# A routed block's rows stored unnormalised, with their reciprocal roots beside them

## The reference

```python
def rmsnorm(x, g):
    xf = x.astype(jnp.float32)
    y = xf * lax.rsqrt(jnp.mean(xf * xf, axis=-1, keepdims=True) + EPS)
    return (y * g.astype(jnp.float32)).astype(x.dtype)

x = x + hierarchical_moe(rmsnorm(x, norm2_g), ...)      # then a last rmsnorm

def expert_block(args):
    e, rows_tok, rows_w = args
    xb = tok[rows_tok]                       # rows of the normed x, chosen by the router
    a = xb @ w_gate[e]
    u = xb @ w_up[e]
    y = (jax.nn.silu(a) * u) @ w_down[e]
    return (y * rows_w[:, None].astype(y.dtype)).astype(tok.dtype)
```

## Time and profile before

| | |
|---|---|
| median of 3 runs | 1619.41 us (1617.6 to 1621.46) |
| time of the profiled execution | 1620.07 us |
| its span | 1618.3 us |
| PE busy | 1515.8 us (94%) |
| DVE, ACT, POOL busy | 662.3, 512.4, 473.8 us |
| read from HBM | 302.84 MB |
| weight chunks of 2048 KB to the arena, the ring, hT | 49, 43, 1 |

### The profile page before, as it was taken

How to read it: one execution, slowest core, us unless ns; L and a number is a source line. 1 busy time by engine, 2 the same in 40 slices (tenths; PEclk the granted TensorE clock), 3 DMA queues, 4 the chain that set the end, 5 groups by cost and what they waited for, 6 DMA issues and landing times.

```text
span 1618.3 us, 18890 instructions
## 1 busy us (share of the span) xinstructions
PE 1515.8 (94%) x7408; PEld 1010.7 (62%) x7409; DVE 662.3 (41%) x1090; ACT 512.4 (32%) x912; POOL 473.8 (29%) x250
## 2 busy tenths in 40 slices
PE   7999999999999999999998999898799998998986
PEld 6975566887778888878866766456344343433432
DVE  3155565223643333321135678573423232232324
ACT  5236566222543333321245433424111111111112
POOL 4441114444434444444424363432100000000100
PEclk9999999999999999999999999999799999999998
DMA  7323001222232223223223221118899999999994
GB/s 301 110 96 90 2 1 36 96 91 91 79 116 98 98 94 102 91 92 99 96 79 111 96 73 67 51 54 336 355 429 427 430 430 430 426 429 429 422 429 183
DMA packets 44680, 306.12 MB, mean 189 GB/s; under 512 B 6272, under 2 KB 6400, under 8 KB 31920
## 3 DMA queue, kind: packets, MB, share of 16 engines
q1 hardware_dynamic: 39664, 290.56, 46.2%
q0 software_dynamic: 4352, 12.25, 2.0%
q10 hardware_dynamic: 576, 2.10, 0.4%
HBM read 302.84 MB, written 4.19 MB: 190 GB/s over the span
## 4 chain that ended last, share of the span: by engine, by line
PE 73%; DMA 11%; DVE 9%; ACT 3%; issue 2%; POOL 0%; SPq 0%; ACTq 0%; DVEq 0%; POOLq 0%
PE banks L402 26%; PE banks L1059 11%; DMA ring<-experts 11%; PE banks L432 10%; PE banks L1087 3%; PE banks L2175 3%; PE banks L923 2%; PE banks L412 2%; PE banks L2104 2%; PE banks L2120 2%; PE banks L1094 2%; PE banks L780 1%; PE banks L2087 1%; PE banks L781 1%; PE banks L2091 1%
## 5 line engine op out<-in xcount | busy, mean ns | idle before, releaser
L365 POOL TENSOR_TENSOR arena_r<-ring,arena_r 128x1024 fp32r<-128x1024 f32 x143 | 352.1, 2467 | 449.9 <-ACT arena_r L350 449.9
L402 PE MATMUL banks<-hT_r,arena_r 128*128 128x512 f32 x1216 | 388.7, 391 | 5.4 <-POOL arena_r L365 4.0
L350 ACT ACTIVATE arena_r<-ring 128x1024 fp32r<-128x1024 f32 x143 | 150.7, 1059 | 466.8 <-PE banks L402 305.0
L402 PE MATMUL banks<-arena_r 128*128 128x512 f32 x800 | 293.0, 391 | 0.0
L402 PEld LDWEIGHTS banks<-hT_r,arena_r 128*128 128x128 f32 x1216 | 228.2, 188 | 59.5 <-issue 9.2
L1059 PE MATMUL banks<-ring,arena 128*64 128x512 f32 x720 | 226.1, 616 | 19.9 <-DMA ring<-experts 17.0
L432 PE MATMUL banks<-arena_r 128*128 128x512 f32 x784 | 188.3, 394 | 2.2 <-POOL arena_r L365 1.8
L1059 PEld LDWEIGHTS banks<-ring,arena 128*64 128x64 f32 x720 | 73.0, 142 | 157.0 <-issue 157.0
L432 PEld LDWEIGHTS banks<-arena_r 128*128 128x128 f32 x784 | 147.0, 188 | 38.1 <-POOL arena_r L365 3.5
L402 PEld LDWEIGHTS banks<-arena_r 128*128 128x128 f32 x800 | 150.2, 188 | 32.9
L1670 DVE TENSOR_TENSOR resid<-resid,banks 128x1024 f32<-128x1024 f32 x64 | 75.2, 1217 | 139.5 <-PE banks L1094 139.5
(11 more groups left out here) (435 smaller groups left out, 1888.1 us busy)
## 6 DMA issues: line engine op xcount, KB each, us to landing
arena<-experts SPq DMA_DIRECT2D x49, 2048.0 KB, 16.4
ring<-experts SPq DMA_DIRECT2D x43, 2048.0 KB, 16.3
ring<-stream SPq DMA_DIRECT2D x162, 512.0 KB, 3.7
ring<-experts SPq DMA_DIRECT2D x4, 1024.0 KB, 9.4
resid<-x ACTq DMA_DIRECT2D x4, 512.0 KB, 5.7
grow<-grows POOLq DMA_DIRECT2D x4, 512.0 KB, 6.8
rows<-arena POOLq DMA_DIRECT2D x4, 512.0 KB, 11.4
hT<-experts SPq DMA_DIRECT2D x1, 2048.0 KB, 16.1
```

The source lines that it names most:

```text
L350: nc.scalar.activation(parts(name, m)[:, 0, :], tile(tile_n), ACT.Copy).then_inc(S["w_high"], 1)
L365: nc.gpsimd.tensor_tensor(w[:, 1, :], tile(tile_n), plain(w[:, 0, :]), ALU.subtract).then_inc(S["w_low"], 1)
L402: last = nc.tensor.matmul(pb[:, bank, :], w[:, a, k * P:(k + 1) * P], b[:, k, :], start=(k == 0 and part == 0), stop=(k == ND - 1 and part ...
```

## The change

The rows are stored as they are in X, so ACT's scaling into `xn` is left out and POOL stores tile i as soon as `wo2_x` says that it is summed. The reciprocal roots go to a second tensor in HBM, `row_rstd`, 4 bytes for each token, in four stores. Each gather of a block's rows is followed by a gather of its roots into one of two columns, `rstd_at[q]`. ACT gives that column as the scale of the activation, DVE as the scalar of the product. Since the two columns are used in turn, clearing for block b waits for the hidden rows of block b - 2. The first gather waits for eight stores in place of four.

As `xn` is no longer written, place 2 is filled right behind chunk 4. Two waits of SP are gone: the one for the selection ahead of place 1, and the one for the first gather ahead of the places 2 and 3. The signal `xz_ready` becomes one more step of `pool_chain`, and a 64-word buffer becomes one of 48.

```diff
-            pool.wait_ge(S["xz_ready"], 1)
+            pool.wait_ge(S["pool_chain"], 6)
             low_pool(pool, "out2", 2)
 
+            def rstd_out(i):
+
+                pool.wait_ge(S["norm_xn"], 3 * NT + i + 1)
+                pool.dma_start(row_rstd[i * P:(i + 1) * P, :], rms_columns("n4", i)[2]).then_inc(S["rows_st"], 16)
+
             for i in range(NT):
-                pool.wait_ge(S["row_ready"], i + 1)
-                pool.dma_start(rows[i * P:(i + 1) * P, :], xn[:, i, :]).then_inc(S["rows_st"], 16)
+                pool.wait_ge(S["wo2_x"], i + 1)
+                pool.dma_start(rows[i * P:(i + 1) * P, :], X[:, i, :]).then_inc(S["rows_st"], 16)
+                if i:
+                    rstd_out(i - 1)
+            rstd_out(NT - 1)
+            pool.memset(rstd_at[0][:, :], 0.0)
+            pool.memset(rstd_at[1][:, :], 0.0)
             pool.wait_ge(S["lg_done"], 1)
             pool.memset(Xg, 0.0).then_inc(S["xg_zero"], 1)
-            pool.wait_ge(S["rows_st"], 16 * NT)
+            pool.wait_ge(S["rows_st"], 16 * 2 * NT)
...
-            def gather(at):
+            def gather(at, q):
 
                 pool.indirect_dma_start(out=Xg, out_offset=None, in_=rows,
                                         in_offset=bass.IndirectOffsetOnAxis(ap=at, axis=0),
                                         bounds_check=T - 1, oob_is_err=False).then_inc(S["xg_in"], 16)
+                pool.indirect_dma_start(out=rstd_at[q][:, :], out_offset=None, in_=row_rstd,
+                                        in_offset=bass.IndirectOffsetOnAxis(ap=at, axis=0),
+                                        bounds_check=T - 1, oob_is_err=False).then_inc(S[f"rstd_in{q}"], 16)
 
             def cleared(b):
 
+                if not isinstance(b, int) or b >= 2:
+                    pool.wait_ge(S["ex_hid"], b - 1)
                 pool.wait_ge(S["x_tr"], b * 2)
...
             first_in(3)
             first_in(4)
+            spare_in(2)
             sp.wait_ge(S["w_used"], last_of_chunk(0) + 1)
             first_in(0)
...
             spare_in(0)
-            sp.wait_ge(S["sel_ready"], 1)
             spare_in(1)
             sp.wait_ge(S["lg_done"], 1)
             sp.wait_ge(S["norm_xn"], 4 * NT)
-            sp.wait_ge(S["xg_in"], 16)
-            spare_in(2)
             spare_in(3)
...
-            def scale_row(i):
-                act.wait_ge(S["norm_xn"], 3 * NT + i + 1)
-                nc.scalar.activation(xn[:, i, :], X[:, i, :], ACT.Copy, scale=rms_columns("n4", i)[2]).then_inc(S["row_ready"], 1)
...
-            def gate_act(b):
-
+            def gate_act(b, q, turns):
+
+                act.wait_ge(S[f"rstd_in{q}"], turns * 16 + 16)
                 act.wait_ge(S["ex_gate"], b + 1)
-                nc.scalar.activation(sil, pb[:, 0, :], ACT.Silu).then_inc(S["ex_sig"], 1)
+                nc.scalar.activation(sil, pb[:, 0, :], ACT.Silu, scale=rstd_at[q][:, 0:1]).then_inc(S["ex_sig"], 1)
...
-                TT(sil, sil, pb[:, 1, :], ALU.mult).then_inc(S["ex_hid"], 1)
+                STT(out=sil, in0=pb[:, 1, :], scalar=rstd_at[q][:, 0:1], in1=sil, op0=ALU.mult, op1=ALU.mult).then_inc(S["ex_hid"], 1)
```

More of the change, by code:

```diff
@@ L145 @@
 up_gelu up_g ple_mm ple_ev pg_mm pg_sig in2_lin in2_conv in2_f z_ready f_in flt_mm flt_act flt_dve
-mixed tf_mm tf_act prod_ready y_ready xz_ready combined yh_dve pool_chain hn_sq_f hn_sq_h hn_ms hn_rt hn_y
-wo2_mm wo2_x n4_tr n4_ev_dve n4_ev_act rt_lg rt_g rt_exp row_ready gate_half rows_st xg_zero slot_ready sel_ready rank_mm counts_out
+mixed tf_mm tf_act prod_ready y_ready combined yh_dve pool_chain hn_sq_f hn_sq_h hn_ms hn_rt hn_y
+wo2_mm wo2_x n4_tr n4_ev_dve n4_ev_act rt_lg rt_g rt_exp rstd_in0 rstd_in1 gate_half rows_st xg_zero slot_ready sel_ready rank_mm counts_out
 over_ready x_tr x_ev_dve x_ev_act ex_gate ex_up ex_down ex_sig ex_hid h_tr h_ev y_hi y_lo spread p_ready placed added
@@ L201, in build @@
         at_in = [sb(f"at_in{q}", [P, 1], I32) for q in range(2)]
+        rstd_at = [sb(f"rstd_at{q}", [P, 1]) for q in range(2)]
         at_tok, at_p = sb("at_tok", [P, 1]), sb("at_p", [P, 1])
-        sb("to_line", [P, 64])
+        sb("to_line", [P, 48])
         ring = sb("ring", [P, RING, 1024])
@@ L212, in build @@
         rows = nc.dram_tensor("rows", (T, D), F32).ap()
+        row_rstd = nc.dram_tensor("row_rstd", (T, 1), F32).ap()
         def col(name, a=0, w=1):
@@ L632, in second_pool @@
             pool.wait_ge(S["flt_dve"], 8)
-            TT(x0t[:, :, :], x0t[:, :, :], by_channel(rsum_b), ALU.mult).then_inc(S["xz_ready"], 1)
+            TT(x0t[:, :, :], x0t[:, :, :], by_channel(rsum_b), ALU.mult).then_inc(S["pool_chain"], 1)
             for n, g in enumerate(SIGNAL_ORDER):
@@ L668, in second_pool @@
                     pool.wait_ge(S["idx_in"], 2)
-                gather(idx[:, BLOCKS * b:BLOCKS * b + 1])
+                gather(idx[:, BLOCKS * b:BLOCKS * b + 1], b % 2)
             pool.wait_ge(S["ex_up"], SPARE[3] + 1)
@@ L685, in second_pool @@
                             pool.sem_inc(S["gathers"], 1)
-                            gather(at_in[q][:, 0:1])
+                            gather(at_in[q][:, 0:1], q)
                             pool.wait_ge(S["y_lo"], turn * 4 + 2 * (N_PAIR + q))
@@ L1251, in second_act @@
             norm_root(1)
-            scale_row(0)
             x_turned(1)
             norm_root(2)
-            scale_row(1)
             x_turned(2)
@@ L1260, in second_act @@
             logits_out(0)
-            scale_row(2)
             logits_out(1)
-            scale_row(3)
             act.wait_ge(S["rt_g"], 1)
@@ L1294, in second_act @@
             for b in range(N_PAIR):
-                gate_act(b)
+                gate_act(b, b % 2, b // 2)
                 if b + 1 < N_PAIR:
@@ L1314, in second_act @@
                             rows_act(turn * 2 + (N_PAIR + q))
-                            gate_act(turn * 2 + (N_PAIR + q))
+                            gate_act(turn * 2 + (N_PAIR + q), q, turn + N_PAIR // 2)
                             hidden_act(turn * 2 + (N_PAIR + q), at_p[:, 0:1])
@@ L1484, in second_dve @@
             L(TT(even[:, 0, :], even[:, 0, :], odd[:, 0, :], ALU.add))
-            dve.wait_ge(S["xz_ready"], 1)
+            dve.wait_ge(S["pool_chain"], 6)
             dve.wait_ge(S["tf_act"], 21)
@@ L1649, in spread_rows, with pair_hidden @@
                 last.then_inc(S["spread"], 1)
-            def pair_hidden(b):
+            def pair_hidden(b, q):
                 dve.wait_ge(S["ex_up"], b + 1)
                 dve.wait_ge(S["ex_sig"], b + 1)
-                TT(sil, sil, pb[:, 1, :], ALU.mult).then_inc(S["ex_hid"], 1)
+                STT(out=sil, in0=pb[:, 1, :], scalar=rstd_at[q][:, 0:1], in1=sil, op0=ALU.mult, op1=ALU.mult).then_inc(S["ex_hid"], 1)
             def rest_of_y(b, p):
@@ L1706, in second_dve @@
                     add_pair(b - 1, (0, 1, 2))
-                pair_hidden(b)
+                pair_hidden(b, b % 2)
                 if b + 1 < N_PAIR:
@@ L1730, in second_dve @@
                             spread_rows(at_tok[:, 0:1])
-                            pair_hidden(b)
+                            pair_hidden(b, q)
                             rest_of_y(b, at_p[:, 0:1])
```

## The result

The changed kernel takes 1631.21 us (median of 6 runs, 1628.33 to 1634.18) against 1620.43 us for the kernel before (6 runs), a ratio of 1.0069 with a 95% interval of 1.0054 to 1.0083. It is slower by 0.69%, some 11 us; 1620.1 was predicted, in a range up to 1626. The profiled execution took 1630.09 us, its span is 1628.2.

A forecast was written before the change was run, and what follows sets the result against it. The prediction took weight transfers to bound the expert loop; -1.1 + 0.2 + 1.2 + 0.3 + 0.1 = +0.7 us on the profiled 1620.07 gave 1620.8, or 1620.1 us against the runs' median of 1619.41, range 1616.5 to 1626.

The forecast's parts named there:

- most likely case: The forecast itself, whole kernel: 1620.1 us, within the 0.2% that cannot be told from no change; chance 0.66 together with Case D.
- case A: Rival: pair 0 starts late, as root stores or first gather reach their bound; +5.6 to +6.3 us, about 1625.5; chance 0.14.
- step (b): Stores of rows and roots ahead of the first gather, beside a busier stream: cost 0.2 us, up to 7.
- step (c): First gather now meets the tail of the load stream, delaying pair 0: cost 1.2 us (0 to 6.3).
- the gain of 1.1 us: Expert loop: earlier fill removes only the backlog before the loads issued at pair 0's down product; 1.1 us (1.0 to 1.3).
- Step (d): Sixteen more 4-byte root gathers, 14 in the loop's saturated stretch: cost 0.3 us, far bound 17 us.
- case C: Rival: 4-byte gathers eat into the loop's saturated stretch; 17 us at the far bound, 1636.5, half that 1628; chance 0.08.
- (a): ACT loses four scalings of 128x1024, 4.5 us in all, none delaying the chain: worth 0.
- (e): Clearing's wait for hidden rows of pair b-2 ends about when the transposes do, which POOL awaits anyway: 0.
- (f): DVE's product gets a scalar, 0.750 for 0.686 us, bare only in the last pair: cost 0.1 us.
- Case B: Rival: the earlier fill's whole 9.8 us of transfer come off the end, 1609.6 us; chance 0.12.
- Case D: Rival: queue held up elsewhere, early fill does not come, old schedule stays; 1619.9, no change; chance 0.66 together with the forecast.

## Why the prediction was wrong, point by point

**The sum and its sign.** The most likely case, within 0.2% and up to 1626, did not come. What came is case A, pair 0 late by 10.8 us, where the prediction had called more than 3 us a sign of being wrong: the first gather lands at 1156.8, over 4 us after 1145.9, as that case asks. But it is later than its price of 1625.5, which lets either step (b) or step (c) reach its bound and counts on the gain of 1.1 us.

**Step (b) failed.** It is the term "Cost 0.2 us" for the stores of the rows and roots, which counted a small store by its packets: one for each engine and one to close. The count was right. The page shows 4992 packets in POOL's queue, 640 more for 20 more transfers (4 stores, 16 gathers), so 32 each, 16 of them closing ones:

```profile
q0 software_dynamic: 4992, 12.26, 2.3%
```

The rule of the Trainium skill ("DMA: Bandwidth & Descriptors", "SWDGE descriptor pipeline") that small pieces share a packet is thus borne out. The price was not in the packets. Four stores of 512 bytes hold the transfers down for 13 us in two pieces, to 53 and 145 GB/s; the gather is issued 1149.42 - 1141.49 = 7.9 us later by the chain, 8.1 counted from the first sum, and not 0.2. The far bound of the step, 7 us, had about this size, and its landing at 1148.5 is where the last store did land (1148.4), but that is luck: it took a packet for each root and a stream that keeps moving, where the stream stood. The count of packets rules that mechanism out, and the stores with 64 bytes have the same count without the stop.

**Step (c) was too small in size.** The gather beside the stream's tail was put at 1.2 us, in bounds of 0 to 6.3. With both places early and no stops it is 6.72 - 4.45 = 2.3 us; in the changed kernel 7.34 - 4.46 = 2.9, probably since the stops push more of the stream into it. That it comes from place 3's pieces is shown, by one profile: with place 3 behind the gather it is 4.41 again.

**The gain of 1.1 us did not show.** The reading that the earlier fill could not give 9.8 us held: with the stops cured, both early and the old order differ by 0.0004, where 9.8 us would be 0.006. But the 1.1 us cannot be seen either: the loop's part is 425.1 against 424.8 us, in one profile each, and the four kernels that have only unread stores added to the kernel before, and nothing changed in the loop, lie between 424.0 and 425.9. Transfers rested ahead of pair 0's half gate product as predicted (share 0.15 from 1157 to 1165.6). The smallest landing in the loop, though, was predicted at about 7.8 us and is 9.5 in the changed kernel, and 9.9 with both early and no stops, not below the 9.0 of the old order. The bytes give an estimate of what was gained: in the 32 us from 2 us before pair 0's gate product the kernel with both early moves 282 GB/s, 9.0 MB, and the old order 408 GB/s, 13.1 MB. The 4.0 MB between them are nearly the two chunks (4.2 MB) that the first already holds, so it is ahead by some 0.4 us of transfer and not by 1.1.

**Step (d) held as far as can be seen.** The sixteen gathers of roots were put at 0.3 us in the loop. There the kernels with 4-byte gathers take 425.1 and 425.2 us and the old order with 64-byte ones 424.8, against 424.5, all within the spread of the profiles. The 17 us of case C are ruled out. The prediction had named for that case what the Trainium skill ("DMA: Bandwidth & Descriptors", "Specifications") says of transfers under 512 bytes, that they fall below line rate as the engine reads, modifies and writes. It gives no price, and here 4-byte stores at a pitch of 64 bytes cost nothing that the time shows, and the loop with 4-byte gathers is at most 0.7 us longer. Whether that rule lies behind the cost of neighbouring writes no run tells.

**Steps (a), (e), (f)** cannot be seen in the time: with stops, early fill and shifted addresses out, pair 0 starts 0.4 us earlier than in the kernel before and the time is the same.

**Case B** fell: no version was 9.8 us faster. **Case D** fell: SP issued early.

In sum, against the kernel before: 8.1 (stops ahead of the gather) + 2.9 (its landing) + 0.6 (loop) - 1.5 (the tail behind pair 15's gate product, 42.9 us against 44.4) - 0.2 (the part before) = 9.9 us, which is the difference of the spans. The tail goes with the granted clock: in some profiles, that of the kernel before among them, the clock is at 1.2 in place of 2.4 GHz for some 3.4 us about the end of the last wait for a chunk, and the next 32 products take 8.69 in place of 7.09 us. It is not tied to the change: the same tail of 44.4 to 44.6 or 42.7 to 43.1 us turns up in kernels on either side.

What stays open: whether the stop comes from several engines writing into the same 64 bytes or from one engine's own neighbouring writes. The dense store has both, the spaced one has neither. Nor is it shown that 64 bytes are the limit: no smaller pitch was tried, and the dense store also puts all its writes into 512 bytes, the spaced one into 8 KB. And why 64 bytes of address slow the loop was not looked into.

## What to carry to other kernels

Price a transfer by what it writes, not only by its bytes and packets: a column of 4-byte words, one from each partition, laid side by side in HBM, held every transfer of the core down for six to seven microseconds (53 and 145 GB/s for 430), and a pitch of 64 bytes, or 64 bytes each, cured it. When an edit moves tiles about, keep the addresses of the big ones, or measure the shift by itself; here it was worth about 0.2%, more than any term of the prediction's sum. Bringing a fill forward need not bring its transfer time: here it was 9.8 us of transfer and no gain that the time shows, since the next loads wait for places which PE gives back at its own pace.

## What the runs showed of the hardware

A store of 512 bytes as 128 words of 4 bytes took 14.7 to 24.0 us to land beside loads, and over 7 us all transfers together moved 53 GB/s, where a full stretch moves about 430, while the engines' share read 0.91. The page of a profile can thus show full engines that move an eighth. Four such stores added to the kernel before left 56 GB/s from 1122 to 1129, and the same writes 64 bytes apart 384, against 388 without any. The unused buffer of 64 words in front of the ring does something: with 48, and so everything behind it 64 bytes lower in each partition, the same loads ran at 424 to 426 in place of 428 GB/s, and the kernel before took 0.19% longer (0.07 to 0.30).
